# Splitting the diagonal-block step of VectorE's prepare work into two slots of a hand-written plan

## What is computed

```
l_mat = einsum('nbhid,nbhjd->nbhij', kb, kc) * decay_strict
sol = triangular_solve(eye + l_mat, rhs, lower=True, unit_diagonal=True)
attn_intra = einsum('nbhid,nbhjd->nbhij', qc, kc) * decay_incl
```

## Time and profile before

| what | value |
|---|---|
| median of 3 runs | 1899.73 us (1896.98 to 1901.27) |
| the profiled execution, its own time | 1899.6 us |
| its span | 1897.4 us |
| PE busy | 1807.1 us, 95% of the span |
| DVE busy | 911.5 us, 48% |
| ACT busy | 660.9 us, 35% |
| POOL busy | 276.7 us, 15% |
| mean granted clock of TensorE | 0.987 of full speed |

### The profile page before, as it was taken

One profiled execution on the slowest core, in us unless ns is written; L12 is line 12 of the kernel. 1 busy time (PEld: TensorE's weight loads), 2 busy tenths in 40 slices (PEclk: granted clock), 3 DMA queues, 4 the chain that ended last, 5 costly groups with the idle time before them and its releaser, 6 DMA issues.

```text
span 1897.4 us, 25274 instructions
## 1 busy us (share of the span) xinstructions
PE 1807.1 (95%) x10174; PEld 1445.0 (76%) x10174; DVE 911.5 (48%) x1595; ACT 660.9 (35%) x1211; POOL 276.7 (15%) x421
## 2 busy tenths in 40 slices
PE   5799999999999998999999999999999889999999
PEld 2367888888787877788888888877876566688887
DVE  1244443556424565555565553764365544453333
ACT  4322332223234444444434336422344333222211
POOL 0000000000003355476100003111000100210000
PEclk9799999999999999999999999999999999999999
DMA  8794111223215554565444437667542222652332
GB/s 302 238 321 127 56 56 56 63 71 90 72 56 177 171 172 138 163 186 151 144 124 135 119 103 219 215 209 212 152 121 85 89 78 84 246 187 100 122 122 100
DMA packets 198684, 267.12 MB, mean 141 GB/s; under 512 B 37072, under 2 KB 135625, under 8 KB 197161
## 3 DMA queue, kind: packets, MB, share of 16 engines
q1 hardware_dynamic: 175241, 192.74, 33.5%
q0 software_dynamic: 15552, 58.62, 9.4%
q10 hardware_dynamic: 7776, 14.16, 2.0%
HBM read 221.96 MB, written 43.52 MB: 140 GB/s over the span
## 4 chain that ended last, share of the span: by engine, by line
PE 82%; DVE 6%; DMA 4%; ACT 4%; issue 3%; POOL 0%; SPq 0%; ACTq 0%; DVEq 0%; POOLq 0%
PE psum L1611 23%; PE psum L1613 21%; PE psum L1612 21%; PE psum L1916 2%; PE psum L1759 1%; PE psum L1710 1%; PE psum L1708 1%; DVE L_upper L1185 1%; DVE w_lo L1091 1%; PE psum L1936 1%; DMA w_raw_mod<-w_mod_dram 1%; PE psum L1903 1%; PE psum L1604 1%; PE psum L1716 1%; ACT w_hi L759 1%
## 5 line engine op out<-in xcount | busy, mean ns | idle before, releaser
L1091 DVE TENSOR_TENSOR w_lo<-w_raw,w_hi 128x1024 fp32r<-128x1024 f32 x232 | 289.1, 1248 | 642.4 <-ACT w_hi L759 642.0
L759 ACT ACTIVATE w_hi<-w_raw 128x1024 fp32r<-128x1024 f32 x232 | 245.5, 1058 | 863.4 <-PE psum L1613 774.4
L1611 PE MATMUL psum<-h_hi,w_hi 128*128 128x512 f32 x1152 | 473.1, 411 | 22.5 <-DVE w_lo L1091 20.3
L1613 PE MATMUL psum<-h_hi,w_lo 128*128 128x512 f32 x1152 | 453.4, 394 | 0.0
L1612 PE MATMUL psum<-h_lo,w_hi 128*128 128x512 f32 x1152 | 453.0, 393 | 0.0
L1611 PEld LDWEIGHTS psum<-h_hi,w_hi 128*128 128x128 f32 x1152 | 218.4, 190 | 83.9 <-DVE w_lo L1091 21.6
L1613 PEld LDWEIGHTS psum<-h_hi,w_lo 128*128 128x128 f32 x1152 | 218.0, 189 | 49.3
L1612 PEld LDWEIGHTS psum<-h_lo,w_hi 128*128 128x128 f32 x1152 | 219.0, 190 | 36.3
L1161 DVE SCALAR_TENSOR_TENSOR conv_acc<-conv_in,convw,conv_acc 128x772 f32<-128x772 f32 x96 | 98.2, 1023 | 3.4
L1611 PE MATMUL psum<-w_hi,m_hi 128*128 128x512 f32 x256 | 99.6, 389 | 0.0
L1612 PE MATMUL psum<-w_lo,m_hi 128*128 128x512 f32 x256 | 99.6, 389 | 0.0
(11 more groups left out here) (306 smaller groups left out, 2753.7 us busy)
## 6 DMA issues: line engine op xcount, KB each, us to landing
w_raw<-w_in_dram SPq DMA_DIRECT2D x168, 512.0 KB, 4.0
w_raw_mod<-w_mod_dram SPq DMA_DIRECT2D x64, 512.0 KB, 5.7
w_raw_modg<-w_mod_dram POOLq DMA_DIRECT2D x32, 512.0 KB, 4.5
w_raw<-w_out_dram SPq DMA_DIRECT2D x32, 512.0 KB, 3.6
gate_scratch<-gate_stage ACTq DMA_DIRECT2D x48, 256.0 KB, 2.5
w_raw<-w_proj_a_dram SPq DMA_DIRECT2D x16, 512.0 KB, 4.2
w_raw<-w_proj_b_dram SPq DMA_DIRECT2D x16, 512.0 KB, 3.4
gates<-gate_scratch POOLq DMA_DIRECT2D x32, 256.0 KB, 4.1
```

Of the source, the lines that this page charges most:

```text
L759: act.activation(part(whi[i % 2], p), part(place, p), ACT.Copy).then_inc(S("w_hi"), 1)
L1091: dve.tensor_tensor(part(wlo[i % 2], p), part(raw_of(n)[0], p), part(whi[i % 2], p).bitcast(f32), ALU.subtract).then_inc(S("w_lo"), 1)
L1611: pe.matmul(out_ap, lh, rh, start=first, stop=False, skip_group_check=shared)
L1613: return pe.matmul(out_ap, ll, rh, start=False, stop=last, skip_group_check=shared)
```

## The change

DVE's diagonal-block step is cut in two and taken out of `gram` and `qk`. Slot at+5 ("lower") does the four copies of the lower direction, slot at+7 ("upper") the four of the upper direction and the transpose. PE and ACT do nothing in these slots. SP's store of the blocks moves from at+6 to at+8. The next item's `gram` also waits for the semaphore `diagonal`, since `L` is now read for longer.

```diff
-            for m, k in ((0, "kt"), (1, "decay"), (2, "gram"), (3, "qk"), (9, "at"))[:5 if lat else 3]:
+            for m, k in ((0, "kt"), (1, "decay"), (2, "gram"), (5, "lower"), (7, "upper"), (3, "qk"), (9, "at"))[:7 if lat else 5]:
...
-                    if kk == u["at"] + 6:
+                    if kk == u["at"] + 8:
                         sp.wait_ge(S("diagonal"), i + 1)
...
-            def negated_blocks(i):
-
-                if i:
+            def negated_blocks(i, d):
+
+                if i and not d:
                     dve.wait_ge(S("block_in"), 16 * i)
-                for d in (1, 0):
-                    dve.wait_ge(S("L"), 2 * i + d + 1)
-                    for q in range(4):
...
+                dve.wait_ge(S("L"), 2 * i + d + 1)
+                for q in range(4):
+                    own = slice(32 * q, 32 * q + 32)
+                    neg = consts[own, NEG32 + 32 * d:NEG32 + 32 * d + 32].unsqueeze(1).to_broadcast([32, 4, 32])
+                    dst = UPPER[own] if d else DIAG[own, 0]
+                    ins = dve.tensor_tensor(dst, LL[own, d, :, own], neg, ALU.mult)
+                if d:
+                    ln(ins)
+                    dve.transpose(DIAG[:, 1].rearrange("p u n -> p (u n)"), UPPER[:].rearrange("p u n -> p (u n)")).then_inc(
+                        S("diagonal"), 1)
...
                         if i:
                             dve.wait_ge(S("l_out"), 16 * i)
+                            dve.wait_ge(S("diagonal"), i)
...
-                    if not u["lat"]:
-                        negated_blocks(i)
+                elif k in ("upper", "lower"):
+                    negated_blocks(i, k == "upper")
...
-                    negated_blocks(i)
```

## The result

The changed kernel took 1878.03 us in the median of four runs (1873.67 to 1879.51), against 1898.36 us for the kernel before (1891.83 to 1901.27, four runs): a ratio of 0.9908, with a 95% interval of 0.9888 to 0.9927. The profiled execution took 1878.7 us, its span is 1876.5. The forecast was 1880.3, within 1875.5 to 1887.5.

The account below looks back on a forecast made before the run. PE, busy 95% of the span, was taken as the bound, losing time to w_lo waits and lower clock. 15.6 + 6.3 - 1.0 - 0.1 - 1.5 = 19.3 us off 1899.6 gave 1880.3, range 1875.5 to 1887.5.

Parts of the forecast that it names:

- The bound, and where the waits stand: PE, busy 95% of the span, waits six times for w_lo behind bursts of gram, qk and diagonal blocks: 15.6 us.
- Where the slots fall: By slot // 4, w_lo passes all eight copies at items 4, 5, 8, 9; only half at 6 and 10.
- Items 4, 5 and 9: Waits of 1.40, 1.64 and 2.63 us all go, and no later w_lo becomes late.
- Item 8: The 5.54 us wait before p21 goes; a new wait of 1.0 us stands in front of p22.
- Items 6 and 10: Waits of 2.74 and 1.67 us just vanish with half the burst moved; 0.1 us is kept.
- The masks: w_lo beside POOL's masks takes 0.8 us more, absorbed or already counted; masks up to 1.2 us later, no cost.
- The clock: Lower clock behind waits of 2.74, 5.54 and 2.63 us, none behind 1.67; all 6.3 us come back.
- Context items: Both halves move one piece later and the store two slots later; cost zero.
- The start of the scan: The later store delays the first scan load and then L, for which PE waits; cost 0 to 2.6, taken 1.5 us.
- Rival 1: The stall moves by one piece at items 8 and 9, waits about 2.5 us each; 1887.7 us, chance 0.09.
- Rival 2: Every block copy pays for a whole POOL operation, 1.29 us each; slower, 1904.5 us, chance 0.03.
- Rival 3: No change, w_lo being held by w_hi or a late raw load; about 1899 us, chance 0.06.

Follow-up runs that it names:

- no_copies: The kernel before with the eight diagonal-block copies left out for items 1 to 11; 1873.66 us in one run.
- one_early: The changed kernel with both halves of the block step in one place, slot at+5; 1877.9 us in one run.
- early_unit: The changed kernel with SP's loads of L and the inverted blocks for the scan issued one slot earlier, L first; 1876.38 us, median of four runs.
- store_late: The kernel before with only SP's store of the blocks moved from at+6 to at+8; 1895.63 us in one run.
- before_again: The kernel before, unchanged, run once more; 1892.42 us in one run.
- after_again: The changed kernel, unchanged, run once more; 1874.18 us in one run.

## Why the prediction was right, point by point

- *The bound, and where the waits stand.* Right. All six waits were behind a burst of copies, and no_copies has none.
- *Where the slots fall.* Right, and the step that carried most. The reading by slot // 4 gave items 6 and 10 their half burst; one_early confirmed it by bringing back just those two waits.
- *Items 4, 5 and 9.* Gone, as reckoned.
- *Item 8.* The wait of 5.54 us went; the new one in front of p22 was 0.50 us, where I had 1.0. The burst took 6.5 us for my 6.7, and PE spent 7.0 us in p21 (724.5 to 731.5) for my 6.5, since item 9's `kt` falls into it too, which I had left out.
- *Items 6 and 10.* Right, with a gap of about 0.3 us in front of p16 for my 0.1 (the eight transposes of `at` began at 688.70 and the next matmul at 689.81, 1.11 us later; at item 8, where nothing was late, this took 0.79, from 727.27 to 728.06).
- *The masks.* `w_lo` and POOL took turns as supposed; no one waited for the later mask. POOL's pair of masks at item 8 took 3.53 us for 2.60.
- *The clock.* 6.3 us came back against the one execution I worked from, so the sum against that execution was right. As a term of the program it was too sure: the same kernel lost 3.1 us in another. The rule I drew from four waits, that over 1.67 us it falls and up to there it is free, didn't hold either way: 2.66 us was followed by 1.00, and 1.46 us, in early_unit, by the lower clock.
- *Context items.* Cost zero, as forecast.
- *The start of the scan.* The size was near, +1.06 us for my +1.5, but partly by luck. That the later store holds the first scan load was right. The step that failed is that PE pays for this delay as it stands: in store_late `L` was issued 1.3 us nearer to PE's arrival and PE did not wait longer. POOL's load, which I had put out of account as "long after", was issued within 0.5 us of the scan's first load. And the 1.7 us of lower clock behind the wait was not in the sum at all.
- *Rival 1* (the wait moves by a piece) happened at item 8 with 0.5 us only. *Rival 2* needed 1.2 us per copy; L1184's copies from 640 to 797 us take 0.74 and 0.54 in the mean:

```profile
L1184 DVE TENSOR_TENSOR L_diagonal<-L,consts 32x128 f32<-32x128 f32 x32 | 23.7, 742 | 0.3
L1184 DVE TENSOR_TENSOR L_upper<-L,consts 32x128 f32<-32x128 f32 x32 | 17.2, 537 | 0.4
```

  *Rival 3*, a late raw load, did not show.

The sum was 19.3 us. In the profiled executions 20.9 us are gone (1899.6 to 1878.7): 21.3 in the stage, 2.5 ahead of it by chance, and 2.9 given back behind it, of which 1.7 is the clock. Of the 21.3, 15.1 are waits for `w_lo`, 6.3 the clock and -1.1 the wait at the scan; the last 1.0 is in none of these terms. That the time came within 2.3 us of the forecast is in part luck, since the 2.5 by chance and the 2.9 given back nearly cancel, and the 6.3 are those of one execution: from before_again to after_again the stage is 18.1 us shorter.

## What to carry to other kernels

Read an engine's program at its own grain: a step moved by k-tiles moves nothing on an engine that drains its slots once per piece, and what matters is which due operation it passes. When an engine off the critical path hands out what the bound engine needs next, look at what is queued ahead of that operation, and count it with what it costs beside its neighbour: most of this wait (9.5 of 15.6 us) was DVE taking turns with POOL's block steps. A stall taken out ahead of a transfer can make that transfer the next wait, as here at the scan.

## What the runs showed of the hardware

A single w_lo beside the two masks shows the turns plainly, here at item 4 of the changed kernel, DVE and then POOL:

```profile
643.69 1.94 DVE L1091 TENSOR_TENSOR w_lo<-w_raw,w_hi 128x1024 fp32r<-128x1024 f32 x1
```

```profile
643.25 3.52 POOL L601 TENSOR_TENSOR decay<-decay,consts 128x512 f32<-128x512 f32 x2 [1.22 <-DVE decay L1212]
```

`w_lo` takes 1.94 us for the 1.2 of most others, and the masks 3.52 for 2.60: the three operations fill 3.52 us, near the 3.8 that they would take one after the other, and far from the 2.6 that they would side by side. In no_copies the pair of masks takes 3.53 or 3.54 us at four items and 2.54 to 2.56 at the other four. That agrees with what the Trainium skill says in "SBUF — State Buffer", section "SBUF: two separate sides", of VectorE operations with two inputs in SBUF.

The granted clock, where it fell, fell to 0.5 (1.2 GHz), and each fall cost about 1.7 us or twice that. Its cause isn't the length of the wait alone: behind a wait of 2.66 us it stayed at 1.00, behind one of 1.46 us (early_unit, whose next 8 us have 0.79) it fell, and the changed kernel's wait at the scan was followed by 0.79 once and, in after_again, where it was longer, by 1.00. The scan's first product is 32 small matmuls, which no run separates from the wait ahead of them. What decides it stays open.
